# Moving a doubled attention slot two units later, and the order of three VectorE steps after it

## The reference, cut to what matters

```
for each layer:
    modulated input -> ONE combined projection (queries, keys, values of A, B, C; indexer)
    A: dilated sliding-window attention, 6 heads of 64
    B: top-k attention, 6 heads of 64: an indexer scores the keys, only the best are kept
    C: differential attention, 4 heads: softmax map 0 minus lambda times softmax map 1
       (a relative-position bias is added to the logits of all)
    heads concatenated -> ONE output projection -> residual, layer norm
    squared-ReLU MLP -> residual, layer norm
```

## Time and profile before

| | |
|---|---|
| median of 3 runs | 1391.57 us |
| lowest, highest | 1389.1, 1395.66 us |
| the profiled execution: its own time | 1389.1 us |
| its span in the trace | 1387.3 us |
| mean granted clock of TensorE | 0.982 |
| TensorE matmul busy | 1285.6 us, 93% |
| VectorE busy | 551.5 us, 40% |
| second half of the attention stage, layer 0 | about 290 to 390 us |
| the same, layer 1 | about 959 to 1058 us |

### The profile page before, as it was taken

One profiled execution on the slowest core, in us unless ns is written; L12 is line 12 of the kernel. 1 busy time (PEld: TensorE's weight loads), 2 busy tenths in 40 slices (PEclk: granted clock), 3 DMA queues, 4 the chain that ended last, 5 costly groups with the idle time before them and its releaser, 6 DMA issues.

```text
span 1387.3 us, 23104 instructions
## 1 busy us (share of the span) xinstructions
PE 1285.6 (93%) x8038; PEld 811.2 (58%) x8038; DVE 551.5 (40%) x1416; ACT 258.0 (19%) x647; POOL 60.4 (4%) x265
## 2 busy tenths in 40 slices
PE   5989898887999999999999999998899999999998
PEld 2544356544566666666656444665456667767775
DVE  1104688875664111011121088777756411101113
ACT  0111123322213111000013112433220311100001
POOL 1000000000001000000001000000000100000000
PEclk9999999998999999999999999999989999999999
DMA  9989979989943777976863586999995366676663
GB/s 352 244 271 269 283 261 377 363 269 345 319 167 114 273 264 268 330 287 241 334 227 140 199 300 214 342 366 318 347 350 189 132 243 212 220 285 212 212 212 137
DMA packets 189567, 363.80 MB, mean 262 GB/s; under 512 B 22913, under 2 KB 140361, under 8 KB 187787
## 3 DMA queue, kind: packets, MB, share of 16 engines
q1 hardware_dynamic: 155040, 345.62, 71.9%
q10 hardware_dynamic: 34410, 16.70, 5.0%
HBM read 354.17 MB, written 58.40 MB: 297 GB/s over the span
## 4 chain that ended last, share of the span: by engine, by line
PE 67%; DVE 8%; SPq 7%; DMA 7%; DVEq 4%; issue 3%; ACT 2%; ACTq 0%
PE psf L1055 22%; PE psf L1489 19%; SPq L519 7%; DMA ring<-in_tiles 5%; PE psf L1355 4%; PE psf L1401 3%; DVEq L1675 3%; DVE m L1672 3%; PE psf L1472 3%; PE psf L1072 2%; PE psf L1290 2%; PE psf L1102 1%; PE psf L1247 1%; PE psf L1134 1%; DVE S L1723 1%
## 5 line engine op out<-in xcount | busy, mean ns | idle before, releaser
L1055 PE MATMUL psf<-hT,ring 128*128 128x320 f32 x1184 | 329.3, 437 | 2.1 <-DMA ring<-in_tiles 1.9
L1055 PEld LDWEIGHTS psf<-hT,ring 128*128 128x128 f32 x1184 | 224.3, 191 | 110.1 <-issue 13.7
L1489 PE MATMUL psf<-big,ring 128*128 128x320 f32 x1024 | 278.6, 433 | 2.7 <-DVE big L1910 2.1
L1489 PEld LDWEIGHTS psf<-big,ring 128*128 128x128 f32 x1024 | 193.6, 190 | 88.6 <-issue 5.0
L1910 DVE TENSOR_TENSOR big<-sq 128x320 f32<-128x320 f32 x64 | 31.5, 492 | 244.9 <-ACT sq L1024 244.6
L1587 DVE TENSOR_SCALAR rstd<-psf,adaT 128x256 f32<-128x256 f32 x32 | 15.4, 482 | 247.9 <-PE psf L1489 233.2
L1362 PE MATMUL psf<-hT,ring 128*128 128x320 f32 x224 | 68.7, 450 | 13.3 <-DVE nmxi L1792 13.3
L1672 DVE MAX8 m<-workbuf 64x8 f32<-64x1032 f32 x64 | 78.5, 1227 | 3.6
L1674 DVE MATCH_REPLACE8 workbuf<-m,workbuf 64x1032 f32<-64x1032 f32 x64 | 77.4, 1209 | 0.0
L1247 PE MATMUL psf<-big,qs 128*32 128x512 f32 x512 | 68.0, 621 | 7.3 <-DVE sel L1879 7.1
L982 ACT ACTIVATE sq<-xT 128x320 f32<-128x320 f32 x32 | 15.0, 470 | 319.7 <-DVE xT L1591 319.7
(11 more groups left out here) (192 smaller groups left out, 1242.1 us busy)
## 6 DMA issues: line engine op xcount, KB each, us to landing
ring<-in_tiles SPq DMA_DIRECT2D x272, 512.0 KB, 4.5
big<-in_cache_a SPq DMA_DIRECT2D x64, 768.0 KB, 7.4
out_cache_a<-in_cache_a SPq DMA_DIRECT2D x64, 768.0 KB, 5.7
big<-in_pool_bk SPq DMA_DIRECT2D x128, 192.0 KB, 4.8
big<-in_pool_bv SPq DMA_DIRECT2D x128, 192.0 KB, 6.2
big<-in_pool_cv SPq DMA_DIRECT2D x192, 64.0 KB, 5.8
big<-in_pool_ck SPq DMA_DIRECT2D x128, 64.0 KB, 4.3
big<-in_pool_ck ACTq DMA_DIRECT2D x128, 64.0 KB, 5.4
```

Source lines behind the costliest of these rows:

```text
L1055: ins = pe.matmul(ps[:, 0:T], ring[:, s, k, :], rhs[:, k, :], start=k == 0, stop=k == KD - 1)
L1489: ins = pe.matmul(bank[6 + m % 2][:, 0:T], ring[:, s, k, :], uT[:, KD * q + k, :], start=q + k == 0, stop=q == 3 and k == KD - 1)
```

## The change

The table `SLOTS` gives the second item to unit 13 instead of unit 11: units 11 and 12 now have items 11 and 12, unit 13 has items 13 and 14, unit 14 has item 15. The loops of all engines read the table, so all follow. In units 7 to 14 VectorE's three steps change their order: `item_scale` of this item comes before `place_outputs` and `item_out`, where it came after them. In units 0 to 6 the order stays. No instruction is added or removed.

```
-SLOTS = [*([n] for n in range(11)), [11, 12], [13], [14], [15], [ITEMS]]
+SLOTS = [*([n] for n in range(13)), [13, 14], [15], [ITEMS]]
...
                     item_read(slots[0])
                     read_outputs(u)
+                    item_scale(slots[0])
                     if n + 1 >= len(LATE):
                         place_outputs(u)
+                    if slots[0]:
                         item_out(slots[0] - 1)
-                        item_scale(slots[0])
-                    else:
-                        item_scale(slots[0])
-                        if slots[0]:
-                            item_out(slots[0] - 1)
+                    if n + 1 < len(LATE):
                         place_outputs(u)
```

## The result

| | before | after |
|---|---|---|
| median | 1389.1 us (7 runs, 1383.08 to 1395.66) | 1402.07 us (7 runs, 1400.32 to 1408.59) |
| ratio to before | | 1.010, 95% interval 1.0079 to 1.0121 |
| the profiled execution: its own time, its span | 1389.1, 1387.3 us | 1395.17, 1393.4 us |
| mean granted clock | 0.982 | 0.976 |

The change makes the kernel 1% slower, 13.0 us between these medians. The forecast was + 5.4 us; the direction is right, the size is less than half, and the median lies just above the range. The profiled execution of after is the quickest of all that were timed, so by itself it shows a loss of only 6.1 us. Two more profiles of the same kernel stand among the experiments.

What follows compares the result with a forecast made beforehand. In the changed stage the page stream, some 12 us a unit, was taken to race TensorE. Losses of 3.0 us in layer 0 and 2.4 in layer 1 gave + 5.4 us, 1397.0 us on the median, range 1388.0 to 1402.0.

Steps and rivals of the forecast that it cites:

- The stage and the first wait: Unit 12 would wait for a `cv` page, 3.3 us in layer 0, and start at 347.0 and 1014.5.
- V12: Moment when the values of unit 12 have landed: 346.9 in layer 0, 1014.4 in layer 1.
- one sign of being wrong: Values of unit 11 in layer 1 coming after 1005 would mean the cover there was gone.
- the cover: In layer 1 unit 12's wait for pages hides the new order's 2.6 to 2.8 us delay, with 1.2 us to spare.
- The delay in units with 4 maps: The new order delays `place_outputs`, giving 2.6 to 2.8 us at the values of unit 11, covered by waits.
- Order on the later units: Ordinary units lose 0.2 to 0.35 us; the doubled unit gains 0.4 (15.9), the last 0.35 (9.3).
- V13 is 350.8 + 5.1 = 355.9: Landing of unit 13's values in layer 0, from SyncE's last page issue plus its flight; unit 13 would find them there.
- The clock: TensorE runs at 1.2 GHz for a while after a wait: 1.55 us, paid once per layer at unit 12.
- the low clock lasts: Rival: unit 12's wait and the doubled unit's idle time cost each layer 1.5 us more, 1400.0 us; chance 0.22.
- The page stream takes some 12 us a unit: In the attention stage a unit's 4 MiB of pages at 348 GB/s takes 12.05 us, whatever the compute does.

Runs made afterwards that it cites:

- the pair without waits: The kernels before and after, each without pages 4 to 7 of B's keys and values in units 8 to 15: 0.9924 and 0.9942 of before.
- both groups held back: The kernel after, with ScalarE's `ck` pages of unit 15 and its half of the `cv` pages of unit 14 issued later: 1.003 of before.
- the run with narrow pages: The kernel after, with all 8 pages of B's keys and values issued but only 128 of 384 columns of each: 0.9965 of before.

## Why the prediction was right and wrong, step by step

**The stage and the first wait: right.** The values of unit 12 end a wait for a `cv` page at 346.78 in layer 0. The wait is shorter than forecast (2.20 for 3.3 us), because unit 11 itself started at 335.32 and not at 334.2. In layer 1 they start at 1017.79 instead of 1014.5, but the whole layer came 3.7 us late, because layer 0 had lost time; from unit 7 to the landing of V12 it is 54.6 us, before 54.9. For the same reason one sign of being wrong came true without its cause: the values of unit 11 in layer 1 start at 1005.30, past the 1005 that I had named, but unit 12 still waits 3.23 us there, so the cover was not gone.

**The delay in units with 4 maps: right, its size uncertain.** From the values of unit 8 to those of unit 10 layer 0 takes 25.2 us (300.72 to 325.95), before 21.3 (300.30 to 321.56): 4.0 us. At the values of unit 11, counted from unit 7 and without the 2.92 us of wait that before had, it is 3.5, where 2.6 to 2.8 was forecast. But these stretches vary between executions: in the pair without waits the delay at unit 11 is 2.2 and 2.7 us, and in layer 1 of the first profiles it is 0.6, so that the wait at unit 12 there was 3.23 us and not the 1.3 of the forecast. It was covered by the vanished wait, as forecast, and did not reach the stream.

**Order on the later units: right, and better than forecast.** The last unit takes 9.0 us (9.3 forecast), and an ordinary unit loses 0 to 0.2 us (9.20 and 9.36 with the order alone, 9.03 and 9.35 before), where 0.2 to 0.35 was forecast. The order alone gains 0.24%.

**"V13 is 350.8 + 5.1 = 355.9": the step that failed.** I carried the landing of V13 over from the trace of before as if the stream were untouched, and wrote of ScalarE's queue that issuing fewer loads in unit 13 "costs nothing". The point was not unit 13 but unit 12: the second item in unit 11 had held ScalarE's next loads back until 354.12, after SyncE's last page of V13. With it gone they start at 346.79, and V13 lands at 359.57 (351.12 + 8.45), 12.9 us after V12 instead of 9.0. TensorE has 10.4 us of work of its own behind unit 12 (12.92 less the wait of 2.48), so it waits 2.5 to 3.3 us again. Holding the two groups back gives 8 to 9 of 12.2 us back and brings unit 13's pages to 5.9 us of flight: that is shown. What ScalarE issued puts 3.3 us on SyncE's page (8.4 for 5.1 before), and 2.2 to 2.5 of them go when it is held back (6.2 and 5.9). The Trainium skill (DMA: Bandwidth & Descriptors, "Issuing engines are not separate DMA queues") says that DMAs of different issuing engines run on the same 16 DMA engines and interleave. The trace agrees, by these flights.

**The clock: one term too few.** I paid 1.55 us once per layer, at unit 12, and costed the doubled unit at 15.9 us. With both groups held back that is what it takes (15.9 and 16.0), and with no wait for pages at all it takes 14.6. In after it starts right behind a second wait, and takes 16.0 and 14.5, 18.8 and 18.7, 16.4 and 17.4 us in three profiles. The rival "the low clock lasts" was thus the nearest, 1400.0 us against 1402.07; but it had only one wait in it, so it came near for a reason that was in part not its own, and its argument against itself, that a unit lies between wait and doubled unit, fell with the second.

**"The page stream takes some 12 us a unit": right as a number, wrong as a cause.** I read the 12 us as bytes at 348 GB/s. With half of the bytes SyncE's round still takes 12.3 us: its 20 issues are enough to set it. The Trainium skill (DMA: Bandwidth & Descriptors, "Issuing engines are not separate DMA queues") calls the sequencer's time to start a DMA usually small beside the DMA itself. For one page that holds here (some 0.5 us an issue, 1.8 us of flight or more), but not for the stream: in the run with narrow pages the 20 issues alone take the round. In after both limits lie together, and which of them would give way first is not shown.

**What stays open.** With both groups held back the kernel is still 0.3% slower than before (0.1 to 0.5%), 0.5% slower than the order alone, which ran on another chip. The first wait and the clock around it are what is left, by argument; no run separates the two. And each experiment has one profile, so which of its doubled units are typical is not known.

**The best version** is the old table with the new order: 0.9976 (0.9956 to 0.9995) of before, 1389.75 us. It is a little faster than before and 1% faster than after.

## What to carry to other kernels

An engine that issues loads is part of the stream even when its own work is off the path: when work moves, list for every issuing queue which transfers now go out earlier, and what lands behind them. Don't carry a landing time over from the old trace unless all that was in flight beside it is unchanged. And put the long unit where the stream has just been caught up with (here unit 11): it pays for itself in pages, while one that comes two units later is preceded by waits and can start at the low clock (18.8 us for 14.6 at worst).

## What the runs showed of the hardware

- SyncE's round of 20 page issues takes 11.7 to 12.4 us whether a unit's pages are 4 MiB or half of it. The last 64 KB page of the values of units 12 and 13 flies 1.8 and 3.9 us with narrow pages (layer 0), and 5.1 to 8.9 us with full ones in before and after.
- 96 matmuls on one group of columns took 21.04 us (191 records, 0.11 us each), while 64 records of the values, which change between four groups of columns, take 1.95 us (0.03 us each).
- TensorE was at 1.2 GHz for some five sixths of a stretch of 18.8 us (clock 0.58) behind a wait of 3.26 us, while it was busy 17.1 of these 18.8 us. In another execution of the same kernel the same stretch took 16.0 us at 0.79.
